# Gate logits of a hybrid decoder layer: one 512-column product for both parts of the input, the sums folded by VectorE

## The reference, cut to what matters

```python
proj = h @ w_in[l]                        # h: (256, 1024); the last 3072 columns are the gate logits
gates = jax.nn.sigmoid(glog.reshape(B, S, N_BRANCH, D) + b_gate[l])
merged = (gates[:, :, 0] * (y_att @ w_br_att[l])
          + gates[:, :, 1] * (y_conv @ w_br_conv[l])
          + gates[:, :, 2] * (y_xatt @ w_br_xatt[l]))
x = x + merged @ w_out[l]
x = x + moe_ffn(rmsnorm(x, norm_ffn_g[l]), ...)      # 32 experts, top 4
```

## Time and profile before

| | |
|---|---|
| median of 3 runs | 1184.27 us |
| profiled execution, its own time | 1183.07 us |
| span of the profile | 1181.3 us |
| TensorE granted clock | 0.981 of full speed over the span |
| TensorE / VectorE / ScalarE busy | 1105.3 / 392.6 / 245.6 us |
| DMA traffic | 452.13 MB, mean 383 GB/s |

### The profile page before, as it was taken

How to read it: one execution, slowest core, us unless ns; L and a number is a source line. 1 busy time by engine, 2 the same in 40 slices (tenths; PEclk the granted TensorE clock), 3 DMA queues, 4 the chain that set the end, 5 groups by cost and what they waited for, 6 DMA issues and landing times.

```text
span 1181.3 us, 14726 instructions
## 1 busy us (share of the span) xinstructions
PE 1105.3 (94%) x6066; PEld 584.6 (49%) x6066; DVE 392.6 (33%) x650; ACT 245.6 (21%) x388; POOL 4.5 (0%) x10
## 2 busy tenths in 40 slices
PE   9999999999999989898898989898999989998996
PEld 8999999983443333333333333333343333333332
DVE  7768655563222322222222222222222222222222
ACT  5444774432111111111111111111111111111113
POOL 0000000000000000000000000000000000000000
PEclk9999999999999999999999999999999999999999
DMA  9955754689999999999999999999999999999996
GB/s 331 324 179 188 263 168 151 258 326 413 425 424 429 431 432 428 429 434 433 429 427 438 428 428 428 437 429 427 428 437 431 426 431 428 430 431 429 412 423 266
DMA packets 61131, 452.13 MB, mean 383 GB/s; under 512 B 3570, under 2 KB 34535, under 8 KB 40871
## 3 DMA queue, kind: packets, MB, share of 16 engines
q1 hardware_dynamic: 60272, 449.53, 92.1%
q0 software_dynamic: 560, 1.74, 0.5%
q10 hardware_dynamic: 263, 0.34, 0.1%
HBM read 450.53 MB, written 1.06 MB: 382 GB/s over the span
## 4 chain that ended last, share of the span: by engine, by line
PE 49%; DMA 48%; DVE 1%; issue 0%; SPq 0%; ACT 0%; DVEq 0%
DMA dring<-in_w_down_dram 41%; PE bank L1182 19%; PE bank L1557 13%; PE bank L1506 10%; DMA ring<-in_w_gu_dram 7%; PE bank L1451 1%; PE bank L1189 1%; PE bank L1396 1%; PE bank L1277 0%; PE bank L1426 0%; PE bank L1518 0%; PE bank L1460 0%; DMA region_x<-in_mem_dram 0%; PE bank L1623 0%; PE bank L1298 0%
## 5 line engine op out<-in xcount | busy, mean ns | idle before, releaser
L1506 PE MATMUL bank<-ring,region_x 128*64 128x512 f32 x2048 | 456.3, 597 | 7.2 <-DMA ring<-in_w_gu_dram 7.2
L1557 PE MATMUL bank<-dring,region_r 128*64 128x512 f32 x1024 | 247.4, 634 | 55.4 <-DMA dring<-in_w_down_dram 54.9
L1506 PEld LDWEIGHTS bank<-ring,region_x 128*64 128x64 f32 x2048 | 141.0, 137 | 280.1 <-issue 264.3
L1557 PEld LDWEIGHTS bank<-dring,region_r 128*64 128x64 f32 x1024 | 74.2, 145 | 225.6 <-issue 135.1
L1182 PE MATMUL bank<-hT_high,w_high 128*128 128x256 f32 x384 | 109.9, 286 | 0.0
L1182 PE MATMUL bank<-hT_low,w_high 128*128 128x256 f32 x384 | 108.6, 283 | 0.0
L1182 PE MATMUL bank<-hT_high,w_low 128*128 128x256 f32 x384 | 108.6, 283 | 0.0
L755 DVE TENSOR_TENSOR w_low<-ring,w_high 128x2048 fp32r<-128x2048 f32 x38 | 87.0, 2289 | 51.7 <-ACT w_high L488 51.6
L1089 DVE TENSOR_SCALAR region_r<-bank 128x512 f32<-128x512 f32 x32 | 22.1, 692 | 245.2 <-PE bank L1506 245.2
L1108 DVE SCALAR_TENSOR_TENSOR y_parts<-bank,region_r,y_parts 64x512 fp32r<-64x512 f32 x31 | 23.1, 744 | 214.5 <-ACT y_parts L656 214.5
L639 ACT ACTIVATE region_r<-region_r 128x512 f32<-128x512 f32 x32 | 20.1, 630 | 315.3 <-DVE region_r L1089 315.3
(11 more groups left out here) (250 smaller groups left out, 880.1 us busy)
## 6 DMA issues: line engine op xcount, KB each, us to landing
ring<-in_w_gu_dram SPq DMA_DIRECT2D x50, 4096.0 KB, 25.7
dring<-in_w_down_dram SPq DMA_DIRECT2D x58, 2048.0 KB, 24.4
ring<-in_w_gu_dram SPq DMA_DIRECT2D x17, 2048.0 KB, 12.0
ring<-in_w_in_dram SPq DMA_DIRECT2D x26, 1024.0 KB, 6.6
ring<-in_w_gu_dram SPq DMA_DIRECT2D x22, 1024.0 KB, 8.5
dring<-in_w_down_dram SPq DMA_DIRECT2D x11, 1024.0 KB, 11.6
ring<-in_w_out_dram SPq DMA_DIRECT2D x4, 1024.0 KB, 4.8
ring<-in_w_mem_kv_dram SPq DMA_DIRECT2D x3, 1024.0 KB, 11.8
```

Of the source, the lines that this page charges most:

```text
L1506: last = mm(ps[64 * half:64 * half + 64, :], xg[u // 2][:, c, 64 * (u % 2):64 * (u % 2) + 64], ring[:, slot0 + c, k * F + half * 512:k * F ...
L1557: last = mm(ps[64 * half:64 * half + 64, :], lhsT, dring[:, c // 2, at:at + 512], start=(c == 0), stop=(c == KC - 1))
```

## The change

The two parts of the input get one name, so that chunk c of both can be read as one operand of 512 columns (low first, then high). For each chunk one matmul takes the rounded weights times both parts into all 512 columns of a bank, and a second one takes the rest of the weights times the high part into columns 256 to 511. A bank now holds one tile of 128 channels, as two half sums; bank k belongs to tile k. VectorE's `gate_sum(n)` adds the halves (a reduction over pairs 256 columns apart) into `sig`, once for each tile, and the sigmoid reads `sig` and writes it back in place. `gate_sum` stands in VectorE's order ahead of the head work at the group's begin (2g) and ahead of w_low p+4 (2g+1). TensorE waits, for each tile, until VectorE has summed that bank's former tile.

```diff
-    hT_low = rounded("hT_low", [P, KC, S], "dring", 0)
-    hT_high = rounded("hT_high", [P, KC, S], "dring", PIECE)
+    hT_both = rounded("hT_both", [P, 2, KC, S], "dring", 0)
+    hT_low, hT_high = hT_both[:, 0], hT_both[:, 1]
...
         def sigmoid(n):
-            act.wait_ge(pieces_used, N_PROJ + 3 * (n // 2) + n % 2 + 1)
-            if n >= 2:
-                act.wait_ge(merged_sb, n - 1)
+            act.wait_ge(gate_summed, 2 * n + 2)
             for k in range(2):
                 tile = b * 8 + half * 4 + (n % 2) * 2 + k
-                last = act.activation(sig[n % 2][:, k * 256:k * 256 + 256], bank[n % 2][:, k * 256:k * 256 + 256],
-                                      ACT.Sigmoid, bias=b_gate[:, tile:tile + 1])
+                cut = slice(k * 256, k * 256 + 256)
+                last = act.activation(sig[n % 2][:, cut], sig[n % 2][:, cut], ACT.Sigmoid, bias=b_gate[:, tile:tile + 1])
...
+        def gate_sum(n):
+            for k in range(2):
+                if k:
+                    dve.wait_ge(pieces_used, N_PROJ + 3 * (n // 2) + n % 2 + 1)
+                else:
+                    dve.wait_ge(gate_half_done, n + 1)
+                    if n >= 2:
+                        dve.wait_ge(merged_sb, n - 1)
+                dve.tensor_reduce(sig[n % 2][:, k * 256:k * 256 + 256],
+                                  bank[k][:, :].rearrange("p (h t) -> p t h", h=2), AX.X, ALU.add).then_inc(gate_summed, 1)
...
+                if u == 0:
+                    gate_sum(2 * g)
                 if j < HEADS:
                     head_top(j)
...
                     if g == 0:
                         conv_low(2)
+                    gate_sum(2 * g + 1)
                     w_low_part(p + 4)
                     combine(2 * g)
...
         def gate_logits(n):
-            if n < 2:
-                pe.wait_ge(proj_sb, N_PROJ - 1 + n)
-            else:
-                pe.wait_ge(gates_sb, n - 1)
             for k in range(2):
+                if n == 0:
+                    pe.wait_ge(proj_sb, N_PROJ - 1 + k)
+                else:
+                    pe.wait_ge(gate_summed, 2 * n - 1 + k)
+                cut = slice(k * P, (k + 1) * P)
                 for c in range(KC):
-                    last = product(bank[n % 2][:, k * 256:k * 256 + 256], w, (hT_high, hT_low), ...)
-            last.then_inc(pieces_used, 1)
+                    order = ("both", "low") if c == 0 else ("low", "both")
+                    for part in order:
+                        if part == "both":
+                            last = mm(bank[k][:, :], w[0][:, c, cut], hT_both[:, :, c, :], start=(c == 0), stop=(c == KC - 1))
+                        else:
+                            last = mm(bank[k][:, 256:512], w[1][:, c, cut], hT_high[:, c, :], start=False, stop=False)
+                last.then_inc(pieces_used if k else gate_half_done, 1)
```

More of the change, by code:

```diff
@@ L303, in build @@
     sq_done, root_done, exp_done, probsT_sb = sem("sq_done"), sem("root_done"), sem("exp_done"), sem("probsT_sb")
+    gate_half_done, gate_summed = sem("gate_half_done"), sem("gate_summed")
     y_att_sb, gates_sb, router_exp = sem("y_att_sb"), sem("gates_sb"), sem("router_exp")
@@ L1335, in gate_logits @@
             w = parts(N_PROJ + 3 * (n // 2) + n % 2, KC)
-            if n < 2:
-                pe.wait_ge(proj_sb, N_PROJ - 1 + n)
-            else:
-                pe.wait_ge(gates_sb, n - 1)
             for k in range(2):
-                for c in range(KC):
-                    last = product(bank[n % 2][:, k * 256:k * 256 + 256], w, (hT_high, hT_low),
-                                   (slice(None), c, slice(k * P, (k + 1) * P)), (slice(None), c, slice(0, S)),
-                                   c == 0, c == KC - 1)
-            last.then_inc(pieces_used, 1)
+                if n == 0:
[3 more added lines that the diff above has]
+                cut = slice(k * P, (k + 1) * P)
+                for c in range(KC):
+                    order = ("both", "low") if c == 0 else ("low", "both")
[5 more added lines that the diff above has]
+                last.then_inc(pieces_used if k else gate_half_done, 1)
         def branch(g, second):
```

## The result

The changed kernel takes 1187.05 us (median of 13 runs, 1185.37 to 1188.55) against 1183.70 us for the kernel before in the same series (13 runs, 1182.94 to 1184.77). The ratio is 1.0027, 95% interval 1.002 to 1.0035: some 3.2 us slower, by more than the measurement can miss. The forecast was 0.5 us slower, 1184.7 us, with a range of 1182.0 to 1190.0 that holds the measured time. The profiled execution took 1187.04 us, span 1185.3 us. All ratios here are of executions in the fast state (one of the kernel before, of 6304.3 us, in the series of "changed, again" and "conv_low early", is left out).

A forecast was written before the change was run, and what follows sets the result against it. TensorE until the mixer's output product, then the experts' weight stream by DMA, was taken to bound the kernel. Terms: -2.48 + 0.41 + 2.53 = +0.5 us on 1184.27, giving 1184.7 us, range 1182.0 to 1190.0.

The forecast's parts named there:

- the rival of a hidden change: Mixer time doesn't reach the end because the weight stream is full anyhow: 1184.3 us whatever TensorE does; chance 0.10.
- a mixer that ends d later moves the stream and the end by d: At the mixer's end: the experts' full weight stream starts when the output product ends, 261.9 us, so delays carry through.
- the sums: On VectorE: 24 added reductions from PSUM, 0.69 us each, 16.5 us in total, with room for them.
- The rival of the dear reduction: VectorE's strided sums are dear, deciding from 0.82 us each; at 1.09 us net +7.9 us, 1192.2 us; chance 0.18.
- the stalls of the sums: TensorE waits for VectorE's sum of the preceding gate piece: 0.4 us at gate 9, 2.5 us at gate 11.
- what the merged product wins: TensorE's gates: 346.5 ns a chunk in place of 359.4, 12.9 ns less, 192 times: 2.48 us less.
- The rival of no gain: Split operand reads slowly or 512 columns cost two of 256; gate 11's stall stays: +2.6 us, 1186.9 us; chance 0.08.
- that of the weight loads in the open: Weight loads aren't hidden: TensorE wins 23 us, 20.8 us of stalls hand most back, leaving -2.2 us, 1182.1 us; chance 0.01.
- a stall of 2.5 us: TensorE before gate 11 waits for gate 10's tile 0 sum, late behind VectorE's queue; booked as +2.53 us.
- all weight pieces still come in time: Behind gate 11 no weight piece is late; the closest, the output product's third, keeps some 3.7 us of room, from 5.
- The rival of the full gain: No stalls at the gates, so the whole TensorE gain arrives: -2.5 us, 1181.8 us; chance 0.11.
- The likeliest case: Whole kernel: same time within 0.2%, 2.4 us, between borders 1181.9 and 1186.6 us; chance 0.63.

The follow-up runs named there:

- changed, again: The changed kernel, unaltered, measured once more as a base on the same chip: ratio 1.0025 to the kernel before.
- conv_low early: Changed kernel with only the second conv_low moved ahead of w_low of piece 21 and head work in group 0: ratios 1.0013 and, repeated, 1.0015.
- ten spare matmuls: Changed kernel with ten unused 512-column matmuls on TensorE just ahead of its wait at gate 11: ratio 1.0018 to the kernel before.
- four banks: Changed kernel with gate pieces from 4 on alternating between two pairs of banks: ratio 0.9988 to the kernel before.
- sums first: Changed kernel with the sums of the next group's first gate piece moved right behind the group's combine on VectorE: ratio 0.9991 to the kernel before.
- both spare ones: Changed kernel with ten or four unused 512-column matmuls ahead of the wait at gate 11: ratios 1.0018 and 1.0015 to the kernel before.
- the two with sums first and conv_low early: Changed kernel with next-group sums behind the combine and the second conv_low moved ahead, without or with alternating bank pairs from gate 4: ratios 0.9983 and 0.9982.
- three products: Changed kernel with the 512-column product split again into two of 256, sums and waits kept: ratio 1.0032 to the kernel before.
- before with a wait: Kernel before with one added wait: TensorE starts gate 11 only once w_high of the output product's first piece is written: ratio 1.0033.

## Why the prediction was right or wrong

**Right: what bounds the kernel, and that the mixer's end sets the end.** SP's issues of the experts' weights come 2.86 us later up to 406.40 us, which is how much later the output product starts; the rival of a hidden change falls. Behind that the stream varies by itself by about 1 us and more (941.4 to 943.8 us from the output product to the end of the span), which the sentence "a mixer that ends d later moves the stream and the end by d" leaves out. The prediction's own sign, an output product that ends within 1 us of 261.9 us, did not come: it was 2.85 us late.

**Right in size: the sums.** 24 of them, 0.684 us each, as the head's maximum and not as the strided row of 1.09 us. The rival of the dear reduction falls (VectorE by line and shape):

```profile
L925 DVE TENSOR_REDUCE region_r<-bank 128x256 f32<-128x512 f32 x24 | 15.8, 684 | 2.3 <-PE bank L1360 2.2
```

**Right: the stalls of the sums.** Gates 3, 5 and 7 have none, as forecast, though the head work ahead of them was read as 0.9 to 1.2 us and is 2.3, 1.3 and 0.9 us in the trace of before. Forecast 0.4 us at gate 9 and 2.5 us at gate 11; the gaps between starts are 0.61 and 2.69 us, 0.38 and 2.46 us more than a running stream. The chain forecast the sum of gate 10 from T+12.8, where T is the end of gate 9; the first row behind that gate starts at 216.0 us and the sum at 228.96, T+13.0. The sigmoid costs 0.91 us for two out of SBUF, 0.07 more, within the tenth that was allowed.

**Nearly right: what the merged product wins.** Forecast -2.48 us. With every wait removed the stretch is 2.02 to 2.19 us shorter, so the 12.9 ns a chunk, read from the output product's 226.7 ns, came out as about 11. The rival of no gain and that of the weight loads in the open (23 us won) fall; that the former's 1186.9 us is near the measured time is luck, since its mechanism, a product that wins nothing, is not there.

**Wrong: what idle time costs.** The step "a stall of 2.5 us" priced an idle TensorE by its length. In the traces of the changed kernel the half clock behind it adds 1.68 us, the difference to the kernel with ten spare matmuls. This is the largest part of the miss. The experiment in the kernel before, 2.82 us idle and 4.52 us longer, shows that the new products and sums are not needed for it. Spare matmuls were traced once each, and the clock stays up in some traces with the full wait too, so one such trace could be chance; taken together, the low level stands behind five of seven waits of 2.27 to 2.82 us, and in none of the seven traces where TensorE's longest wait was 1.32 us or less (before, four banks, sums first, both spare ones, the two with sums first and conv_low early).

**Wrong: the walk left out conv_low.** The prediction followed the waits for sums and for weight pieces ("all weight pieces still come in time"), and for the early gates said that nothing stood in the way. The second conv_low, which the first branch product needs, sits behind the first sums and the head work. It was 0.6 us early before and is 0.5 us late after; with the restart behind the gap it costs 0.7 to 0.8 us (0.75 and 0.77 in two pairs of traces).

Together, in one trace: -2.1 + 0.4 + 2.5 + 1.7 + 0.7 = 3.2 us, against 3.16 us measured in the stretch. The forecast of 0.5 us had the first three terms. The terms come from different traces, and the median gives 3.2 us as well. The rival of the full gain was the mechanism that the cures bring about, but the changed kernel as it stands never had it.

The likeliest case, within 0.2% of the time before, is not what happened: the measured 1.0027 lies beyond it, on the side of slower, which had a chance of 0.27, and by a mechanism that was not among the rivals for it. The range held it because it reached to 1190.0 us for the dear reduction, which did not happen; that part is luck.

**Left open.** What decides whether the clock falls behind an idle time of 2.3 us: of six traces with one of 2.27 to 2.31 us, four show the low level (the changed kernel twice, three products, conv_low early once) and two don't, one of these with the same code as one of the four. The clock of an unprofiled execution in this stretch is not on record. The times of the changed kernel spread over 3.2 us where those before spread over 1.8, which would fit a fall in some executions and not in others, but in another series the kernel before spread over 3.4 us itself, so the spread shows nothing. For the same reason the 1.7 us is a price for an execution in which the clock falls, not a share of the median that was measured by itself; what the medians show of it is 1.1 and 1.4 us. And from the output product to the end of the span, the three traces with gate products of 256 columns (before, three products, before with a wait) take 941.4 to 941.6 us, the eleven with the merged product 942.1 to 943.8. No experiment was made on that.

## What to carry to other kernels

A product merged from two saves only the fixed part of a matmul (about 11 ns here), and each new dependence on another engine's queue has to be walked to its end before it is booked as free: here 2.5 us of waiting at one gate, with the clock's fall behind it, cost more than 192 saved matmuls won. Where one engine's result frees another's buffer, put it ahead of bulk work that has slack in the order, or give the buffer a second turn; either one turned this change from 3.2 us slower into 1.1 to 1.4 us faster (for the order alone the interval just reaches no change), and with the second late operand moved too, 2 us faster. An idle stretch of a TensorE at full clock can cost more than its own length, as the 2.82 us that cost 4.52 us show; when a wait can't be avoided, compare against the same kernel with spare matmuls in it.

## What the runs showed of the hardware that was not expected

- Behind 2.3 us of idleness, in a TensorE that had been at 1.00 and all but always busy from 140 us on, the granted clock was 0.50 for about 3.4 us and cost 1.7 us, in four of six traces; in the other two, one of the same code, it stayed at 1.00. Behind 2.82 us in the kernel before it fell as well (one trace); behind 1.32 us it stayed at 1.00 (one trace).
- A reduction over pairs that lie 256 float32 columns apart in a PSUM bank takes what one over 256 neighbours takes: 0.684 us for 512 columns in and 256 out, against 0.686 us for 512 in and 2 out.
- A 512-column operand in two runs of 256 costs little or nothing extra: a chunk with it (one product of 512, one of 256) takes 348 ns in gate 0, where the prediction's sum of the two, from a dense operand, is 346.5 ns and three products of 256 took 359.4.
